# Ends of phases without TensorE's drain, and local attention that divides its probabilities before they are turned

## The reference, cut to what matters

```python
def window_gqa(q, k, v, q_c, k_c, v_c, sink, with_ctx):     # 8 query heads, 2 key heads, width 64
    ...
    p_win, p_ctx = joint_softmax([jnp.where(valid, score(qg, k_win), -jnp.inf), score(qg, k_c)], sink_f)
    return values(p_win, v_win) + values(p_ctx, v_c)

def joint_softmax(scores, sink=None):
    ...
    e = [jnp.exp(s - m) for s in scores]
    den = sum(ei.sum(axis=-1, keepdims=True) for ei in e) + jnp.exp(sink - m)
    return [ei / den for ei in e]
```

## Time and profile before

| | us |
|---|---|
| median of 3 runs | 3133.36 (3133.25 to 3134.44) |
| the profiled execution | 3134.17 |
| its span, first to last instruction | 3132.5 |
| PE busy | 3041.2 (97% of the span) |
| VectorE busy | 1706.7 (54%) |
| ScalarE busy | 1143.4 (37%) |
| GpSimd busy | 193.6 (6%) |

### The profile page before, as it was taken

How to read it: one execution, slowest core, us unless ns; L and a number is a source line. 1 busy time by engine, 2 the same in 40 slices (tenths; PEclk the granted TensorE clock), 3 DMA queues, 4 the chain that set the end, 5 groups by cost and what they waited for, 6 DMA issues and landing times.

```text
span 3132.5 us, 45498 instructions
## 1 busy us (share of the span) xinstructions
PE 3041.2 (97%) x17980; PEld 2737.8 (87%) x17980; DVE 1706.7 (54%) x3073; ACT 1143.4 (37%) x1939; POOL 193.6 (6%) x157
## 2 busy tenths in 40 slices
PE   8999999999999999999999999999999999999999
PEld 7999978998898889999999988877777887888887
DVE  5744376334367866763222586547444588665334
ACT  5243254333313544212222433435333236532323
POOL 0011100200020000000000000110100210000000
PEclk8999999999999999999999999999999999999999
DMA  9412311310252024531222552241321521443333
GB/s 303 128 35 100 103 41 28 128 61 28 81 168 68 28 95 148 162 113 56 78 56 64 153 173 86 74 128 41 113 66 38 195 68 55 152 145 91 105 93 101
DMA packets 353388, 309.28 MB, mean 99 GB/s; under 512 B 40670, under 2 KB 329388, under 8 KB 351788
## 3 DMA queue, kind: packets, MB, share of 16 engines
q1 hardware_dynamic: 331022, 240.65, 25.8%
q10 hardware_dynamic: 22174, 65.99, 5.8%
HBM read 272.89 MB, written 33.29 MB: 98 GB/s over the span
## 4 chain that ended last, share of the span: by engine, by line
PE 48%; DVE 7%; ACT 2%; issue 1%; DMA 1%; POOL 0%; ACTq 0%; DVEq 0%; POOLq 0%
PE ps L1106 32%; PE ps L1460 5%; PE ps L1118 4%; DVE space L2669 2%; PE ps L1496 2%; PE ps L1538 1%; PE ps L1524 1%; DVE w_lo L2355 1%; DVE mx L2938 1%; PE ps L1490 1%; PE ps L1556 1%; DMA space<-in_w_mod 0%; DVE space L2802 0%; ACT w_hi L1758 0%; PE ps L1713 0%
## 5 line engine op out<-in xcount | busy, mean ns | idle before, releaser
L1106 PE MATMUL ps<-u_hi,w_hi 128*128 128x384 f32 (+1 forms) x1912 | 556.0, 351 | 5.6 <-issue 2.9
L1106 PE MATMUL ps<-u_hi,w_lo 128*128 128x384 f32 (+1 forms) x1912 | 550.5, 348 | 0.0
L1106 PE MATMUL ps<-u_lo,w_hi 128*128 128x384 f32 (+1 forms) x1912 | 550.3, 348 | 0.0
L2355 DVE TENSOR_TENSOR w_lo<-w_raw,w_hi 128x2048 fp32r<-128x2048 f32 x129 | 297.4, 2306 | 324.3 <-ACT w_hi L1758 320.3
L1106 PEld LDWEIGHTS ps<-u_hi,w_hi 128*128 128x128 f32 x1912 | 346.8, 188 | 28.6 <-issue 7.3
L1106 PEld LDWEIGHTS ps<-u_hi,w_lo 128*128 128x128 f32 x1912 | 349.5, 188 | 18.7
L1106 PEld LDWEIGHTS ps<-u_lo,w_hi 128*128 128x128 f32 x1912 | 349.5, 188 | 17.9
L1460 PE MATMUL ps<-u_hi,w_hi 128*128 128x384 f32 (+1 forms) x816 | 306.9, 376 | 10.2 <-ACT space L2122 7.7
L1758 ACT ACTIVATE w_hi<-w_raw 128x2048 fp32r<-128x2048 f32 x129 | 246.1, 1907 | 156.6 <-issue 66.0
L1460 PE MATMUL ps<-u_hi,w_lo 128*128 128x384 f32 (+1 forms) x816 | 296.2, 363 | 0.2
L1460 PE MATMUL ps<-u_lo,w_hi 128*128 128x384 f32 (+1 forms) x816 | 296.4, 363 | 0.0
(11 more groups left out here) (340 smaller groups left out, 5397.3 us busy)
## 6 DMA issues: line engine op xcount, KB each, us to landing
w_raw<-in_w_in SPq DMA_DIRECT2D x288, 256.0 KB, 3.8
w_raw<-in_w_gate_up SPq DMA_DIRECT2D x176, 256.0 KB, 3.9
space<-in_w_mod SPq DMA_DIRECT2D x40, 1024.0 KB, 5.4
w_raw<-in_w_down SPq DMA_DIRECT2D x114, 192.0 KB, 2.9
w_raw<-in_w_branch SPq DMA_DIRECT2D x64, 256.0 KB, 3.7
w_raw<-in_w_out SPq DMA_DIRECT2D x48, 256.0 KB, 3.7
m_scratch<-space ACTq DMA_DIRECT2D x3, 3072.0 KB, 10.0
space<-in_w_mod SPq DMA_DIRECT2D x16, 512.0 KB, 9.7
```

Source lines behind the costliest of these rows:

```text
L1106: last = nc.tensor.matmul(ps[:, 2 * (t % 2) + b, 0:a1 - a0], wv[w][:, k, j * P:(j + 1) * P], xx[:, k, a0:a1], start=(k == 0 and w == 0 and ...
L2355: V.tensor_tensor(w_lo[slot][:, :], w_raw[slot][:, :], w_hi[slot][:, :].bitcast(F32), ALU.subtract).then_inc(w_lo_done, 1)
```

## The change

**Ends of phases.** A new function tells, for each phase, how many tiles have been counted in `acc_ready` when its last product is done. Where the phase is an attention, or a "gemm" with neither modulation units behind its products (`background`) nor the last phase's square sums, that count takes the place of the drain: TensorE executes no drain there, and whoever waited for `pe_end` waits for `acc_ready` at that count. These are 26 phases, 13 in each layer: the rest of the second gates with the first branch, the queries and values of local attention, the three attentions, the three other branches, the three products of latent attention, and two phases of the SwiGLU network (`down0` and `up1`).

**Local attention.** VectorE takes the reciprocal of one column and multiplies the job's probabilities by it in place; TensorE turns the divided probabilities and waits for `a_normed` instead of `probs_ready`. `rden_wide`, its turning and the product behind the values go; `y_pair` is one copy out of PSUM. On TensorE, even i becomes: fill of the whole `quota[i]`, turning of job i, `value_pair(i - 1)`, and the scores of the next pair follow. On VectorE, odd jobs' `denominators` stand ahead of the maxima, and `y_pair` stands behind `pt_copy`.

```diff
+def last_products(phases, background):
+    out, made = [], 0
+    for index, (kind, _, arg) in enumerate(phases):
+        groups = groups_of(phases[index])
+        for g in groups:
+            made = g.t0 + (2 * KD if g.kind == "close" else g.n * g.nt * (g.halves if g.kind == "fill" else 1))
+        plain = kind == "gemm" and index not in background and groups[-1].name not in SQUARED
+        out.append(made if kind == "attend" or plain else None)
+    return out
...
+        def wait_products(eng, index):
+            if products_end[index] is None:
+                eng.wait_ge(pe_end, products_end[:index + 1].count(None))
+            else:
+                eng.wait_ge(acc_ready, products_end[index])
...
                 self.eng.wait_ge(others_end, 3 * self.n)
-                self.eng.wait_ge(pe_end, self.n)
+                wait_products(self.eng, self.n - 1)
...
                 self.n += 1
-                self.eng.drain().then_inc(pe_end, 1)
+                if products_end[self.n - 1] is None:
+                    self.eng.drain().then_inc(pe_end, 1)
...
                             sp.wait_ge(others_end, 3 * index)
-                            sp.wait_ge(pe_end, index)
+                            wait_products(sp, index - 1)
...
+                    elif kind == "a":
+                        pe.wait_ge(a_normed, n.rden + i + 1)
...
-                    pe.wait_ge(a_rden, n.rden + i + 1)
                     if p:
                         pe.wait_ge(y_copied, job0 + 2 * p)
-                    nc.tensor.transpose(ps[:, 6, P:2 * P], rden_wide[:, p % 2, :],
-                                        ident[:, :])
                     pe.wait_ge(pt_copied, 2 * (job0 + i + 1))
...
                     elif not final:
-                        fill(before(i))
-                    if kind == "a":
-                        if i and not i % 2:
-                            value_pair(i - 1)
-                    elif i:
+                        fill(plan.quota[i])
+                    if kind != "a" and i:
                         values(i - 1)
...
-                    if not final:
-                        fill(plan.quota[i] - (0 if scored else before(i)))
+                    if scored:
+                        fill(plan.quota[i])
                     probs_t(i)
+                    if kind == "a" and i and not i % 2:
+                        value_pair(i - 1)
...
                         own.wait()
-                        half = slice(64 * (i % 2), 64 * (i % 2) + 64)
-                        V.reciprocal(rden_wide[:, i // 2 % 2, half],
-                                     den[:, m:m + 1].to_broadcast([P, 64])).then_inc(a_rden, 1)
+                        own.did(V.reciprocal(rden[:, m:m + 1], den[:, m:m + 1]))
+                        own.wait()
+                        probs = p_slot(kind, map0 + i)[:, 0:len(job_maps(l, kind, *jobs[i])[1]) * P]
+                        V.tensor_scalar(probs, probs, rden[:, m:m + 1], None, ALU.mult).then_inc(a_normed, 1)
...
-                    own.did(V.tensor_copy(y, ps[:, 6, P:2 * P]))
-                    own.wait()
-                    V.tensor_tensor(y, y, ps[:, 6, 0:P], ALU.mult).then_inc(y_copied, 2)
+                    V.tensor_copy(y, ps[:, 6, 0:P]).then_inc(y_copied, 2)
...
+                        if kind == "a" and i % 2:
+                            denominators(i)
                         for j in range(i + 1, min(i + 3, len(jobs)) if i % 2 else 0):
                             maxes(j)
-                        denominators(i)
-                    if kind == "a":
-                        if i and not i % 2:
-                            y_pair(i // 2 - 1)
-                    elif i:
+                        if kind != "a" or not i % 2:
+                            denominators(i)
+                    if kind != "a" and i:
                         finish(i - 1)
...
                     if kind != "d":
                         pt_copy(i)
+                    if kind == "a" and i and not i % 2:
+                        y_pair(i // 2 - 1)
```

More of the change, by code:

```diff
@@ L355, in build @@
     n_closes = sum(kind == "close" for kind, *_ in phases)
+    products_end = last_products(phases, background)
     stack = ExitStack()
@@ L382, in build @@
         esink, rden = sb("esink", [P, 4]), sb("rden", [P, 4])
-        rden_wide = sb("rden_wide", [P, 2, P])
         ssq, rms_d = sb("ssq", [P, 2, HEADS]), sb("rms_d", [P, 2, 2, HEADS])
@@ L540, in build @@
         rstd_d = sem("rstd_d")
-        a_rden = sem("a_rden")
+        a_normed = sem("a_normed")
         c_split, c_total, c_sums, c_mean_ready = sem("c_split"), sem("c_total"), sem("c_sums"), sem("c_mean_ready")
@@ L1572, in tile_t @@
                     n.yt += 1
-                def before(i):
-                    return max(plan.quota[i] // 2, plan.quota[i] - 2) if kind == "a" else plan.quota[i] // 2
                 map0, job0 = n.map, n.job
```

## The result

The changed kernel takes 3140.8 us (median of 14 runs) beside 3134.32 us of the kernel before, run with it on the same chip: a ratio of 1.0021 with a 95% interval of 1.0012 to 1.0029. Two of its 14 runs, of 4276 and 7889 us, fell in a slower state and are left out of the ratio. It is slower by some 6.5 us, just over the 0.2% that can be told from nothing. The forecast was a gain of 2 us, called no change; 3140.8 lies inside the range, on the side that had 0.21. The profiled execution took 3139.6 us (span 3137.9).

The account below looks back on a forecast made before the run. TensorE, busy for 97% of the span, was taken as the bound. Drains -12, saved work -12, old waits -12, latent attention -1.5, new wait +32 and evictions +3.5 made -2: 3131.4 us, range 3121 to 3142.

Parts of the forecast that it names:

- the side that had 0.21: The outcome slower by over 0.2%, given 0.21 from two rivals: slow multiplication (0.10) and drains giving nothing (0.11).
- the rival at 0.81: Local attention: VectorE's 640-column multiplication takes 0.81 us instead of 0.55, costing 12.6 us, 3144 in all; chance 0.10.
- The step from values to scores: Local attention on TensorE: values directly ahead of scores cost one mode change, taken as 0.20 us.
- The new wait: Local attention: TensorE's even turnings wait for VectorE's add, reciprocal and multiplication, +32 us over 40 pairs.
- the sum for local attention: Saved TensorE work -12, old waits -12, new wait +32, evictions +3.5: local attention 11.5 us longer.
- the walk over 40 pairs: Local attention's pairs laid out in code order with the earlier trace's durations, giving the new wait of +32 us.
- the old waits that go: Local attention: TensorE's waits for `rden_wide` and the copies ahead of the values vanish, -12 us, bounds 6.1 and 12.
- The drains: At 26 phase ends TensorE's drain goes and nearly all lost time returns: -12 us, bounds -12.8 and 0.
- late next: Behind removed drains, some next products wait for other operands anyway, keeping some 0.6 us of the 12.8 gain.
- Latent attention: Every second job's fill moves ahead of the values, removing their waits for VectorE's copy: -1.5 us, bounds 0 and -3.
- The likeliest case: The forecast itself: both halves cancel, 3131.4 us, no change that can be told; chance 0.49.
- The rival of "faster": Local attention: VectorE's chain is hidden further than walked, or values ahead of scores cost nothing extra; likeliest 3121, chance 0.30.

Follow-up runs that it names:

- e2: The changed kernel with every drain back, so the attention half alone: 3148.2 us, ratio 1.0045 to the kernel before.
- e4: The changed kernel with VectorE's part of the weight split moved behind the even job's multiplication: 3130.7 us, ratio 0.9988 to the kernel before.
- e1: The kernel before with only the drains half of the change: 3123.91 us, ratio 0.9963 to the kernel before.
- e3: The changed kernel without VectorE's multiplication, probabilities left undivided: 3114.78 us, ratio 0.9936 to the kernel before.
- e5: The kernel before with the drains half and TensorE's new order, division kept as before, a pair's last copy and product later on VectorE: 3117.92 us, ratio 0.9945.

## Why the prediction was wrong

**Right in its steps.** The multiplication took 0.553 us for 640 columns and 0.486 for 512, where 0.55 was taken; the rival at 0.81 falls. The Trainium skill, VectorE: DVE Perf Modes, on the mode that uses both read ports for one tensor, says that an fp32 operation with one tensor operand in SBUF can run at twice the rate of one with two; the trace agrees in direction, 0.486 against the 0.68 of the two-operand split of 512 columns. The step from values to scores is 0.20: the 20 values and the step take 1.24 from 489.47 to 490.71, as forecast. The Trainium skill, TensorEngine Tiling (Array Packing), Key Properties, names a drain at a change of mode; the row agrees with one change. The new wait, counted by starts, is 33 us where 32 was forecast, and the evictions grew by 3.7 by the list, where 3.5 was. The waits for `rden_wide` left the list.

**The step that failed** is the sum for local attention, -12 - 12 + 32 + 3.5 = 11.5 us, from the walk over 40 pairs "with the durations of this trace". It measured 18.7. Of the missing 7.2, 2.9 are the two falls of the clock: the walk let PE run every product at the full clock of a stretch that, before, had no long wait in it. Another 1.5 is the restart. The turning behind a wait takes 0.05 us longer to the values (0.58 for four turnings in e2's rows above, against 0.53 in e4's, where none stands ahead of them), and 30 waits came. One more is the wait itself (33 for 32) and the evictions. For the last 1.8 us the sum itself has a candidate, the old waits that go: by starts the trace of before has 6.5 us ahead of `rden_wide` and 3.3 ahead of the values, 9.8 in all, where the sum took its upper bound, 12.

**The drains** were put at 12 us, and this term failed too, in its overlap. In e1's trace the products directly behind the 26 ends come 11.5 us earlier in all, as forecast (by some 0.5 or more at 17 of them); 8 us further on 8.8 are left. At eight ends, three in layer 0 and five in layer 1, behind layer 1's three attentions among them, the whole gain was gone by then: another wait had taken it. That is the "late next" of the prediction, put at 0.6 of 12.8; it took some 3. In the trace of after the two sums are 11.9 and 8.6. The medians of e1 give 11.8 with an interval of 7 to 16, which holds both.

**Latent attention**, forecast at -1.5 because its waits for VectorE's copy would go, kept them: 1.3 us in 2 places, as in the earlier trace rows. By e2 the new order gave 0.8, and I have no row for how.

**The sum.** -2 forecast, +7.2 in local attention, +3.4 in the drains, +0.7 in latent attention: some 9, against 5.4 between the two profiles and 6.5 between the medians. The profiles differ by most of the rest for other reasons: in layer 1's differential attention the kernel before had a fall of the clock at 2556.2 that after didn't have, 2.0 us in the stages, and in the first 40 us its clock was low for 20.5 us, after's for 10.2, which made 1.2.

**The chances.** The likeliest case was two halves that cancel, and by the medians they nearly do: e1 gives -11.8, e2 +12.5. Their sum of 0.7 is not the 6.5 of both together, but the intervals are wide (7 to 16 and 9.7 to 18.2); the profiled spans give -7.6 and +15.9, a sum of 8.3 beside 5.4. What was mis-sized is a small difference of large terms, 37.5 us taken off and 35.5 put on; "slower" deserved more than 0.21, and it had a mechanism, long waits in a stretch without them, that the rivals didn't contain. The rival of "faster", a chain hidden further than walked, was the least supported: in e3, 26 us go with the multiplication's 39, so two thirds of it are in the open.

## What to carry to other kernels

A new wait of the engine that bounds the kernel can cost more than its length: here restarts of 0.05 us each and, in two places, a lowered clock came on top, and a walk with the durations of a stretch without waits has neither. When a change puts arithmetic ahead of that engine and shortens its own row at the same time, separate the two in the forecast: here the drains and the shorter row alone are worth 17 us (e5), and moving the division, with the order on VectorE that came with it, gave all of it back and 6 more. Look at the whole queue between a releaser and the awaited instruction; changing the places of a copy and a reciprocal in it brought some 5 us with no work removed. And where a stop is taken away, look a few microseconds further: a quarter of what the drains gave was taken back by the next wait.

## What was not expected of the hardware

Behind single waits of 1.8 to 2.8 us (by starts), in a stretch that was otherwise densely filled, TensorE's granted clock went from 2.4 to 1.2 GHz and back, which cost 1.57 and 1.34 us. The same wait on the same work brought a fall in one kernel and none in another. The Trainium skill, TensorE: Matmul & The Clock Gate, on the HAM clock gate, says that the level is set by how busy the array has recently been and has these two values; the records show no third, and no run here shows which wait it answers to. And a PE drain between two phases, behind most of which the profile shows 0.26 us of idle time and behind none more than 0.43, held the products behind it back by some 0.5 us or more at 17 of the 26 ends.
